# A three-layer hybrid network in split fp32: alternating high and low weight products inside feed-forward and gate blocks

## The reference

```python
def swiglu(h, w_gate_up, w_down):
    a, b = jnp.split(h @ w_gate_up, 2, axis=-1)
    return (jax.nn.silu(a) * b) @ w_down
...
    x = x + 0.5 * swiglu(rms_norm(x, ffn1_norm), ffn1_w_gate_up, ffn1_w_down)
    h = rms_norm(x, mix_norm)
    z = h @ w_in
...
    gates = jax.nn.sigmoid(gl + b_gate).reshape(B, S, N_BRANCH, D)
    merged = gates[:, :, 0] * (y_pool @ w_branch_pool) + gates[:, :, 1] * (y_attn @ w_branch_attn)
    x = x + merged @ w_out
    x = x + 0.5 * swiglu(rms_norm(x, ffn2_norm), ffn2_w_gate_up, ffn2_w_down)
```

## Time and profile before

| | us |
|---|---|
| median of three executions | 1469.42 |
| the profiled execution | 1468.62 |
| its span in the trace | 1466.8 |
| TensorE busy | 1453.1 |
| VectorE busy | 984.1 |
| ScalarE busy | 822.9 |
| DMA, share of the 16 engines' span in the weight queue | 54.2% |
| granted TensorE clock, share of full speed, mean | 0.998 |

### The profile page before, as it was taken

How to read it: one execution, slowest core, us unless ns; L and a number is a source line. 1 busy time by engine, 2 the same in 40 slices (tenths; PEclk the granted TensorE clock), 3 DMA queues, 4 the chain that set the end, 5 groups by cost and what they waited for, 6 DMA issues and landing times.

```text
span 1466.8 us, 20973 instructions
## 1 busy us (share of the span) xinstructions
PE 1453.1 (99%) x8088; PEld 1259.9 (86%) x8088; DVE 984.1 (67%) x1596; ACT 822.9 (56%) x1424; POOL 150.0 (10%) x219
## 2 busy tenths in 40 slices
PE   9999999999999999999999999999998999999999
PEld 7888888898888888888888988888886999888887
DVE  6656676666666666656676677666667756778776
ACT  6555556755555546555467646555566555466553
POOL 0200023000000001000050003000069000100000
PEclk9999999999999999999999999999999999999999
DMA  8665565354655556565563446556447333456552
GB/s 286 245 197 188 190 207 171 137 176 169 215 189 193 182 183 207 182 196 190 165 229 137 158 158 225 191 188 193 165 140 252 115 116 133 167 165 226 193 184 97
DMA packets 73683, 267.78 MB, mean 183 GB/s; under 512 B 8176, under 2 KB 8304, under 8 KB 73456
## 3 DMA queue, kind: packets, MB, share of 16 engines
q1 hardware_dynamic: 73296, 265.65, 54.2%
q10 hardware_dynamic: 288, 0.79, 0.1%
HBM read 265.36 MB, written 1.05 MB: 182 GB/s over the span
## 4 chain that ended last, share of the span: by engine, by line
PE 97%; ACT 1%; DMA 1%; DVE 1%; issue 0%; SPq 0%; DVEq 0%
PE bank L550 29%; PE bank L555 15%; PE bank L503 8%; PE bank L504 8%; PE bank L505 8%; PE bank L564 4%; PE bank L565 4%; PE bank L569 4%; PE bank L540 3%; PE bank L534 3%; PE bank L533 3%; PE bank L523 1%; PE bank L712 1%; DMA raw<-w_dram 1%; PE bank L693 1%; PE bank L702 1%
## 5 line engine op out<-in xcount | busy, mean ns | idle before, releaser
L1563 DVE TENSOR_TENSOR wlo<-raw,whi 128x1024 fp32r<-128x1024 f32 (+1 forms) x481 | 579.2, 1227 | 21.0 <-ACT whi L1031 21.0
L1031 ACT ACTIVATE whi<-raw 128x1024 fp32r<-128x1024 f32 (+1 forms) x481 | 498.1, 1050 | 10.3 <-DMA raw<-w_dram 8.1
L550 PE MATMUL bank<-hx,whi 128*128 128x512 f32 x1856 | 470.4, 394 | 0.0
L550 PEld LDWEIGHTS bank<-hx,whi 128*128 128x128 f32 x1856 | 339.7, 188 | 64.5
L555 PEld LDWEIGHTS bank<-hx,wlo 128*128 128x128 f32 x1856 | 253.0, 190 | 18.4
L555 PE MATMUL bank<-hx,wlo 128*128 128x256 f32 x1856 | 258.6, 282 | 0.0
L503 PE MATMUL bank<-whi,hid 128*128 128x512 f32 x536 | 211.2, 394 | 0.2 <-issue 0.2
L504 PE MATMUL bank<-wlo,hid 128*128 128x512 f32 x536 | 209.9, 392 | 0.0
L505 PE MATMUL bank<-whi,hid 128*128 128x512 f32 x536 | 208.7, 389 | 0.0
L1060 ACT ACTIVATE hid<-prod 128x256 fp32r<-128x256 f32 x126 | 52.7, 418 | 169.1 <-DVE prod L1667 109.2
L505 PEld LDWEIGHTS bank<-whi,hid 128*128 128x128 f32 x536 | 100.7, 188 | 21.8
(11 more groups left out here) (259 smaller groups left out, 1600.5 us busy)
## 6 DMA issues: line engine op xcount, KB each, us to landing
raw<-w_dram SPq DMA_DIRECT2D x486, 512.0 KB, 3.8
gain<-g_dram SPq DMA_DIRECT2D x7, 512.0 KB, 4.5
arena<-c_dram SPq DMA_DIRECT2D x2, 768.0 KB, 7.0
cst<-c_dram SPq DMA_DIRECT2D x1, 1056.0 KB, 5.9
out_dram<-x SPq DMA_DIRECT2D x4, 256.0 KB, 2.0
par<-p_dram SPq DMA_DIRECT2D x1, 867.0 KB, 7.6
raw<-w_dram SPq DMA_DIRECT2D x2, 432.0 KB, 3.1
gain<-g_dram ACTq DMA_DIRECT2D x1, 512.0 KB, 4.8
```

The lines of the kernel that those rows point to most:

```text
L550: e.matmul(b[:, :], hi_of(j)[:, k * P:k * P + P], hx[:, k * 2 * S:k * 2 * S + 2 * S], start=k == 0, stop=False, skip_group_check=True)
L1031: e.activation(hi_of(t), raw_of(t), ACT.Copy).then_inc(sem["w_hi"], 1)
L1563: e.tensor_tensor(lo_of(t), raw_of(t), hi_of(t).bitcast(F32), ALU.subtract).then_inc(sem["w_lo"], 1)
```

## The change

Inside a block the order of the sixteen products changes. Before, the eight with `whi` came first and the eight with `wlo` after them. Now the first two with `whi` come first, then one with `wlo` and one with `whi` by turns, and two with `wlo` end the block. Each `wlo` product runs one slice behind (k - 1). The wait for the low split of the tile stands after the second `whi` product, and the inner tick after the fifth `whi` and the fourth `wlo` product, where it stood after the sixth `whi` product. The products, the operands and the last signal are the same.

```diff
--- before.py
+++ after.py
@@ -545,15 +545,18 @@
 
             def wide_block(j, b, tick=None):
 
+
+                low = lambda k: e.matmul(b[:, 0:S], lo_of(j)[:, k * P:k * P + P], hiT(k), start=False, stop=k == KD - 1, skip_group_check=True)
                 E.wait_ge("w_hi", SI[j] + 1)
                 for k in range(KD):
                     e.matmul(b[:, :], hi_of(j)[:, k * P:k * P + P], hx[:, k * 2 * S:k * 2 * S + 2 * S], start=k == 0, stop=False, skip_group_check=True)
-                    if tick and k == 5:
+                    if k == 1:
+                        E.wait_ge("w_lo", SI[j] + 1)
+                    if k:
+                        low(k - 1)
+                    if tick and k == 4:
                         tick()
-                E.wait_ge("w_lo", SI[j] + 1)
-                for k in range(KD):
-                    ins = e.matmul(b[:, 0:S], lo_of(j)[:, k * P:k * P + P], hiT(k), start=False, stop=k == KD - 1, skip_group_check=True)
-                ins.then_inc(sem["tile"], 1)
+                low(KD - 1).then_inc(sem["tile"], 1)
                 if tick:
                     tick()
```

## The result

The changed kernel takes 1471.63 us, the median of 11 executions (1471.15 to 1477.15); the kernel before, run beside it, 1466.14 us (1465.46 to 1471.12). The ratio is 1.0035, with a 95% interval of 1.0024 to 1.0046: slower by some 5 us. The forecast of 1470 us is 1.6 us off, and its range holds the time. The ratio lies inside the 0.5% that was set as the bound of "same", but it is a clear loss and more than the +1.8 us of the sum.

A forecast was written before the change was run, and what follows sets the result against it. TensorE's spacing of matmul starts was taken to bound the kernel. Terms 0 + 1.8 + 0 + 0 gave +1.8 us on the profiled 1468.6 us, so 1470 us, range 1460 to 1480.

The forecast's parts named there:

- What bounds the kernel: Whole kernel: TensorE's spacing from one matmul start to the next sets the time, no transfer or other engine.
- Part 1: All blocks: no instruction added or removed on any engine, settled sum 2.776 us is today's mean block; cost 0.
- Part 2: Order in the 200 feed-forward blocks: a 512- and 256-column pair takes 0.348 us, 0.009 more per block, +1.8 us.
- slow rival: All 232 blocks: spacing never settles, pair 0.353 us, block 2.818, +10 us, 1478.6 us; chance 0.17.
- the sign that the prediction had set: Feed-forward blocks in the profile after: blocks of 2.82 us would show the slow rival right, 2.78 us was forecast.
- wrong in kind: Profile after: a TensorE wait for VectorE's low split, or a lower granted clock, would be this sort of miss.
- Gate blocks: The 32 blocks of the gate stages: they already run unsettled, so the new order costs 0.
- Part 3: Wait for the low split, moved from the 9th to the 3rd product: tightest place leaves 0.16 us; cost 0.
- Part 4: Attention pieces inside gate blocks come 0.25 us later, against 2.66 us of slack; cost 0, without slack 8 us.
- fast rival: All 232 blocks: low products wait only for weight loads, so turns save 0.048 us each, -11 us, 1457.5 us; chance 0.15.

The follow-up runs named there:

- early wait: The kernel before in its old product order, with only the wait for the low split moved behind the second high product: ratio 1.0000.
- 320 columns: Low products of 320 columns instead of 256, in the order of the kernel before (1514.83 us) and in that of the changed kernel (1520.44 us).
- Two and two: The kernel before with two high and two low products by turns in every block: ratio 0.9988, median 1465.80 against 1467.97 us.

## Why the prediction was right, and where it was off

- **What bounds the kernel:** right. No other engine and no transfer came into it; the whole difference is in the starts of the products.
- **Part 1, instructions, 0:** right, the counts and the work of the other engines are the same.
- **Part 2, the order, +1.8 us:** the term that was mis-sized; the runs show some +5 us for it. It took a pair of 0.348 us, nearer to the edges; the pair is 0.353, the slow rival's, near what the mixer's unsettled rows gave (0.351). The reason it had for the lower value, that the two edge spacings cancel, holds only for the first pair of block a: 114 and 232 ns stand there, 0.346 us, and then the second H after an L collects 241. The lone L does not reset the drag. By the sign that the prediction had set, blocks near 2.82 us, the slow rival was right in the pair, but the loss is half of its 10 us. One reason is its count: six lone L stand between two H in a block, not seven. With six pairs of 0.353 and two of 0.347 a block is 2.812 us, which is the mean of blocks a and b to the nanosecond, and not 2.818. The blocks of before take 2.780 us to the nanosecond and not 2.775, so some of the drag was paid already and the settled sum, 2.774, is not "today's mean block". The products behind are 0.01 us shorter than before, and the 32 gate blocks lost 0.5 us and not 1.4. A feed-forward stage measured up to +1.07 us, the five together +4.8.
- **The time itself:** that 1470 lies so near to 1471.6 is in part luck. The sum stood on a profiled execution of 1468.6 us, in whose stage M the clock fell; the kernel before measured 1466.1 beside the changed one. A base 2.5 us too high made up for most of the 3.7 us that the term was short. The lower clock, which the prediction called wrong in kind, came in stage M alone and in the kernel before as well.
- **Gate blocks, 0:** nearly right, +0.21 and +0.25 us for 16 blocks each. They ran unsettled before (0.351 a pair), which fits so small a loss; no experiment changed them alone.
- **Part 3, the wait, 0:** right, shown by the early wait alone and by the row with 0.23 us of slack.
- **Part 4, the side work, 0:** TensorE has no wait at its lines in those stages. It was not taken apart from the order, but both together cost the two mixers only 0.46 us.
- **The fast rival:** fell twice. Where an L kept its 113 or 114 ns, the H behind it took 232 or 233; the one pair of 0.340 (224 and 116 ns) stands once in nearly every block b, and its neighbours cost more. And with 320 columns, where a load has more time, the drag is the same. The rule of the Trainium skill ("TensorE: Matmul & The Clock Gate", "Step-by-step: what each phase is for" and "Back-to-back issue gap"), that loads are pulled ahead and set the spacing together with the products, made the mixed order look better than it is. The trace agrees that loads go out ahead: each starts about when the product in front of its own starts, 110 to 118 ns before an H that stands behind a lone L and 223 to 239 ns before an L behind an H. The load's own duration that the page states (107 ns for 128 columns) is shown by no run here; the load records last 187 to 192 ns and overlap, 120 ns apart in a run of L.

## What to carry to other kernels

When TensorE alone sets the time, add up starts, not busy times, and look at the spacings one by one: here 0.35% hung on some 6 ns per pair. Keep products of equal width together, since the dear step is the one from a short to a long product, and expect the same drag behind a pause of TensorE; where the widths must differ, join the short runs of neighbouring blocks, and try the entry into a long run in pairs. Putting short products into the shadow of long ones gave nothing here, where the short ones already ran at a steady 120 ns.

## What was not expected of the hardware

- Products of one width settle at a constant spacing: 227 ns for 512 columns, 120 for 256, 147 for 320. After a change from a shorter to a longer width they go 233, 236, 228, 233, 231 before they settle, with high weights alone and with high and low ones mixed (28 ns in all); the other way round the first two products give back 7 ns. A pause of 0.17 us between 512-column products was followed by nearly the same row.
- By turns the pattern doesn't settle at all: 232, 118, 241, 120, 235, 114 ns in block a, then the same again. Two and two shows 232, 231 and 233, 236 by turns with L of 112 to 119, which is nearly the settled sum.
- Why the spacings behave so stays open. Shown is that in the changed kernel the change of width brings the drag about: it is gone with equal widths and the same buffers by turns (512 columns: 227 throughout), it isn't the wait, and it isn't the 27 ns that a load has more with 320 columns. How the load and the product play together behind an edge was not taken apart, nor whether the width of what is read or of what is written in the bank counts.
